# A decoder block on one core: bias row written reversed, modulation bias summed in, three steps of one sum on TensorE, weight places reordered

## What is computed

```
mod = silu(c) @ w_ada + b_ada                  # six rows of 1024: sh1, sc1, g1, sh2, sc2, g2
h   = x * (1 + sc1) + sh1
q, k, v = h @ w_in                             # 8 heads of block attention, 8 of dilated attention
y   = concat(rms(attention_a), rms(attention_b)) @ w_out    # every logit gets a bias by distance
x   = layer_norm(ALPHA * x + (1 + g1) * y)
h2  = x * (1 + sc2) + sh2
# PEER: 8 query heads per token, product keys, 16 experts per head
f   = sum over the 128 experts of a token of  gelu(h2 . u_e) * g_e * v_e
out = layer_norm(ALPHA * x + (1 + g2) * f)
```

## Time and profile before

| | |
|---|---|
| time before, median of 3 runs | 843.8 us (842.85 to 845.88) |
| time of the profiled execution | 842.22 us |
| its span in the trace | 840.4 us |
| busy share: TensorE, VectorE, ScalarE, GpSimd | 85%, 67%, 41%, 34% |
| moved by DMA | 327.95 MB, 390 GB/s over the span |
| chain of waits that ended last | DMA of expert rows 43%, TensorE 35%, VectorE 9% |

### The profile page before, as it was taken

How to read it: one execution, slowest core, us unless ns; L and a number is a source line. 1 busy time by engine, 2 the same in 40 slices (tenths; PEclk the granted TensorE clock), 3 DMA queues, 4 the chain that set the end, 5 groups by cost and what they waited for, 6 DMA issues and landing times.

```text
span 840.4 us, 7310 instructions
## 1 busy us (share of the span) xinstructions
PE 712.5 (85%) x2042; PEld 339.2 (40%) x2042; DVE 567.0 (67%) x1289; ACT 343.8 (41%) x998; POOL 286.3 (34%) x260
## 2 busy tenths in 40 slices
PE   5999999889999989998987876887787787878784
PEld 2876854645545535543432322332222222223221
DVE  6775776679768577756666667767576767675445
ACT  0032032266736444435453436343434435343333
POOL 0000000133534435444544443534343444435420
PEclk9999999899999999999999999999999999999999
DMA  9999993299999999999999999999999999999991
GB/s 353 402 421 422 391 414 112 82 375 411 381 413 418 421 420 421 422 421 420 423 421 420 423 421 422 422 420 423 420 421 422 421 422 422 421 422 406 422 422 74
DMA packets 48183, 327.95 MB, mean 390 GB/s; under 512 B 5584, under 2 KB 7952, under 8 KB 9232
## 3 DMA queue, kind: packets, MB, share of 16 engines
q0 software_dynamic: 36864, 268.45, 77.3%
q1 hardware_dynamic: 10544, 58.73, 17.3%
q10 hardware_dynamic: 736, 0.32, 0.1%
HBM read 326.40 MB, written 1.07 MB: 390 GB/s over the span
## 4 chain that ended last, share of the span: by engine, by line
DMA 46%; PE 35%; DVE 9%; ACT 6%; issue 3%; SPq 1%; ACTq 0%; DVEq 0%; POOL 0%
DMA ring<-in_experts,e_all 43%; PE bank L447 19%; PE bank L439 8%; DVE ring L767 4%; PE bank L470 3%; DMA ring<-in_w 3%; DVE acc L870 2%; ACT diag L617 2%; PE bank L544 1%; ACT weight L613 1%; PE bank L525 1%; ACT L609 1%; PE bank L581 1%; SPq L352 1%; PE bank L515 1%
## 5 line engine op out<-in xcount | busy, mean ns | idle before, releaser
L447 PE MATMUL bank<-ring,diag 128*128 128x512 f32 x1024 | 499.3, 623 | 97.6 <-ACT diag L617 97.4
L987 POOL DMA_INDIRECT ring<-in_experts,e_all x256 | 286.1, 1117 | 526.7 <-PE bank L447 341.4
L447 PEld LDWEIGHTS bank<-ring,diag 128*128 128x128 f32 x1024 | 183.9, 194 | 389.7 <-ACT diag L617 225.6
L767 DVE CUSTOM_DVE_ANT_0 ring<-ring,T_h 128x1024 f32<-128x1024 f32 x128 | 156.7, 1225 | 113.4 <-DMA ring<-in_experts,e_all 113.4
L767 DVE CUSTOM_DVE_ANT_0 ring<-ring,h 128x1024 f32<-128x1024 f32 x128 | 156.6, 1224 | 96.0 <-DMA ring<-in_experts,e_all 95.8
L609 ACT ACTIVATE gel<-pre 128x1 f32<-128x1 f32 x256 | 51.8, 203 | 327.3 <-DVE pre L767 326.6
L617 ACT ACTIVATE diag<-consts,weight 128x128 f32<-128x128 f32 x256 | 102.8, 401 | 8.4
L613 ACT ACTIVATE weight<-gel,g_all 128x1 f32<-128x1 f32 x256 | 75.4, 295 | 9.3
L870 DVE SCALAR_TENSOR_TENSOR acc<-ring,cact,acc 128x512 f32<-128x512 f32 x70 | 52.6, 752 | 3.2
L439 PE MATMUL bank<-ring,hT_yT 128*128 128x512 f32 x80 | 39.9, 655 | 1.7 <-DMA ring<-in_w 1.6
L470 PE MATMUL bank<-hT_yT,lnw 128*128 128x256 f32 x128 | 31.0, 404 | 1.1 <-DVE hT_yT L846 1.1
(11 more groups left out here) (150 smaller groups left out, 527.2 us busy)
## 6 DMA issues: line engine op xcount, KB each, us to landing
ring<-in_w SPq DMA_DIRECT2D x30, 1024.0 KB, 14.5
lnw<-in_w SPq DMA_DIRECT2D x6, 1024.0 KB, 16.7
ring<-in_experts,e_all POOLq DMA_INDIRECT x256, 15.0
H_s<-in_w SPq DMA_DIRECT2D x3, 1024.0 KB, 25.3
mod<-in_w SPq DMA_DIRECT2D x2, 1024.0 KB, 26.6
H_s<-scratch SPq DMA_DIRECT2D x1, 2048.0 KB, 26.6
mod<-in_b_ada_r SPq DMA_DIRECT2D x1, 2048.0 KB, 23.3
lnw<-in_ln SPq DMA_DIRECT2D x1, 2048.0 KB, 11.1
```

Of the source, the lines that this page charges most:

```text
L447: last = nc.tensor.matmul(tile_sum(t)[n], diag[:, i % DIAGS, :], ring[:, RING_AT[i], D + CH * n:D + CH * n + CH], start=(s == 0), stop=(s ...
L767: nc.vector.tensor_tensor_reduce(ring[:, r, 0:D], ring[:, r, 0:D], h2[i // SLOTS], 1.0, 0.0, ALU.mult, ALU.add, pre[:, i % PAIR:i % PAIR + ...
L987: nc.gpsimd.indirect_dma_start(ring[:, r, :], None, A["experts"], bass.IndirectOffsetOnAxis(ap=e_all[:, i:i + 1], axis=0)).then_inc(slot_i ...
```

## The change

- **Bias by distance.** VectorE writes the row reversed, the read back starts one element later and goes straight to `toep`, and VectorE reads `toep` backwards along its last axis. The eight `tflip` matmuls and ScalarE's eight copies are gone.
- **Modulation bias.** GpSimd clears `mod`; a 16 KB DMA puts b_ada in partition 0; GpSimd adds 1 to three of its rows. The first step of each sum from chunk 4 on adds that row (a SCALAR_TENSOR_TENSOR in place of a TENSOR_SCALAR), so the sum over partitions contains it once. The step `madd` becomes a copy on ScalarE.
- **Chunk ada 2.** Its slices 3, 6 and 7 leave VectorE. TensorE multiplies them as they are, with the matching column of `cact` as moving operand, 12 matmuls (`modk`) into the bank of `modc` 0, which is opened by one matmul of zeros.
- **Places and order.** `mod` is no longer a place; `H_s` is. Chunks, loads and steps have a new order. ScalarE issues its small loads later, most of them after the bias row is written.

```diff
@@ -66,18 +66,19 @@
 EXP_PIECE = 7
 
 
-STREAM = [("ada", 0), ("ada", 2), ("in", 0), ("ada", 1), ("ada", 3), ("in", 1), ("ada", 4), ("ada", 5), ("ada", 6), ("in", 2),
-          ("in", 3), ("ada", 7), ("in", 4), ("ada", 8), ("ada", 9), ("in", 5), ("out", 0), ("ada", 10), ("out", 1), ("q", 0),
+STREAM = [("ada", 0), ("ada", 2), ("in", 0), ("ada", 1), ("ada", 3), ("in", 1), ("ada", 4), ("in", 2), ("in", 3), ("ada", 5),
+          ("in", 4), ("ada", 6), ("ada", 7), ("ada", 8), ("ada", 9), ("in", 5), ("out", 0), ("ada", 10), ("out", 1), ("q", 0),
...
-LN_PLACE, MOD_PLACE, HANKEL_PLACE = 4, 5, 6
-W_PLACES = [0, 1, LN_PLACE, 2, 3, MOD_PLACE, 3, 1, 2, 0, 3, 1, LN_PLACE, HANKEL_PLACE, 2, 1, 2, 3, LN_PLACE, 3]
+LN_PLACE, H_PLACE = 4, 5
+W_PLACES = [0, 1, LN_PLACE, 2, 3, H_PLACE, 1, 0, 2, 3, LN_PLACE, H_PLACE, 1, 3, H_PLACE, 2, 1, 3, LN_PLACE, 3]
...
+BY_PE = {2: (3, 6, 7)}
...
+NARROW = [4, 5, 6, 7, 0, 1]
+WIDE = [2, 3] + NARROW
...
-    [("qkz", 0, 0), ("qkz", 0, 1), ("qkz", 1, 0), ("wsum", 0), ("bias",), ("qkz", 1, 1), ("modp", 0), ("wsum", 2), ("modc", 0), ("qkh", 0, 0), ("qkh", 0, 1), ("wsum", 1), ("modp", 1),
-       ("qkh", 1, 0), ("wsum", 3), ("modc", 1), ("qkh", 1, 1), ("qk", 0, 0), ("qk", 0, 1), ("qk", 1, 0), ("qk", 1, 1), ("wsum", 4)]
-    + [("tflip", j) for j in range(8)]
-    + [("wsum", 5), ("wsum", 6), ("S", 0), ("S", 1), ("v", 0, 0), ("wsum", 7), ("Tr", 0), ("Tr", 1), ("qk", 2, 0), ("PV", 0), ("PV", 1),
-       ("modrow", 0), ("madd", 0), ("modrow", 1), ("madd", 1), ("modrow", 2), ("madd", 2), ("wsum", 8), ("qk", 2, 1), ("yT", 0, 0),
-       ("wsum", 9), ("qk", 3, 0), ("modrow", 3), ("madd", 3), ("modrow", 4), ("madd", 4), ("qk", 3, 1), ("wsum", 10), ("S", 2), ("S", 3),
-       ("v", 1, 0), ("wsum", 11), ("modrow", 5), ("madd", 5), ("Tr", 2), ("Tr", 3), ("wo", 0, 0, 0), ("PV", 2), ("PV", 3), ("ny", 0),
+    [("qkz", 0, 0), ("qkz", 0, 1), ("qkz", 1, 0), ("wsum", 0), ("bias",), ("qkz", 1, 1), ("modp", 0)] + [("modk", 2, k) for k in BY_PE[2]]
+    + [("wsum", 2), ("modc", 0), ("qkh", 0, 0), ("qkh", 0, 1), ("wsum", 1), ("modp", 1),
+       ("qkh", 1, 0), ("wsum", 3), ("modc", 1), ("qkh", 1, 1), ("qk", 0, 0), ("qk", 0, 1), ("qk", 1, 0), ("qk", 1, 1), ("wsum", 4),
+       ("S", 0), ("S", 1), ("v", 0, 0), ("wsum", 5), ("qk", 2, 0), ("Tr", 0), ("Tr", 1), ("modrow", 0), ("madd", 0), ("PV", 0), ("PV", 1),
+       ("wsum", 6), ("qk", 2, 1), ("modrow", 1), ("madd", 1), ("yT", 0, 0), ("wsum", 7), ("qk", 3, 0), ("modrow", 2), ("madd", 2), ("wsum", 8),
+       ("modrow", 3), ("madd", 3), ("qk", 3, 1), ("wsum", 9), ("S", 2), ("S", 3), ("modrow", 4), ("madd", 4), ("v", 1, 0), ("wsum", 10),
+       ("modrow", 5), ("madd", 5), ("Tr", 2), ("Tr", 3), ("wo", 0, 0, 0), ("wsum", 11), ("PV", 2), ("PV", 3), ("ny", 0),
...
-        yT = [part.rearrange("p (k c) -> p k c", k=KC) for part in (H_s[:, D:2 * D], hT_yT[:, 0:D])]
...
-        nought = T_h2[0:1, 0:CH]
         h2_0 = sb("h2_0", [P, D])
+        yT = [part.rearrange("p (k c) -> p k c", k=KC) for part in (h2_0[:], hT_yT[:, 0:D])]
...
-        places = [wring[:, n] for n in range(WRING)] + [tile[:].rearrange("p r (k n) -> p (r k) n", n=CH) for tile in (lnw, mod)]
+        places = [wring[:, n] for n in range(WRING)] + [tile[:].rearrange("p r (k n) -> p (r k) n", n=CH) for tile in (lnw,)]
...
-        patches = [tile.rearrange("p (k n) -> p k n", n=CH) for tile in (h2_0[:], xT_y[:, D:2 * D], H_s[:, 0:D], V_x1[:, 1, :])]
...
+        nought = acc[0:1, 3, :]
...
-        consts = sb("consts", [P, 2 * P + TOPK])
-        ident, flip, iota = consts[:, 0:P], consts[:, P:2 * P], consts[:, 2 * P:2 * P + TOPK]
+        consts = sb("consts", [P, P + TOPK])
+        ident, iota = consts[:, 0:P], consts[:, P:P + TOPK]
...
             sp.wait_ge(biasrow_out, 16)
-            shifts = bass.AP(A["scratch"].tensor, 0, [[1, P], [ROW, NH], [1, T]])
-            sp.dma_start(hankel, shifts).then_inc(hankel_in, 16)
-            summed(sp, 2)
+            shifts = bass.AP(A["scratch"].tensor, 1, [[1, P], [ROW, NH], [1, T]])
+            sp.dma_start(toep, shifts).then_inc(hankel_in, 16)
+            filled(sp, ("modc", 0))
+            load(("ada", 4))
+            summed(sp, 0)
+            load(("in", 2))
+            summed(sp, 1)
+            load(("in", 3))
             summed(sp, 3)
-            load(("ada", 4))
             load(("ada", 5))
-            load(("ada", 6))
-            load(("in", 2))
-            summed(sp, 4)
-            load(("in", 3))
-            summed(sp, 5)
-            load(("ada", 7))
             filled(sp, ("qk", 0, 1))
             load(("in", 4))
             filled(sp, ("qk", 1, 1))
-            sp.dma_start(mod[:].rearrange("p r c -> p (r c)"), A["b_ada_r"].broadcast_to([P, 4 * D])).then_inc(rows_in, 16)
-            filled(sp, ("tflip", 7))
+            load(("ada", 6))
+            summed(sp, 4)
+            load(("ada", 7))
+            summed(sp, 5)
             load(("ada", 8))
+            sp.dma_start(x[:], A["x"].rearrange("(t p) c -> p t c", p=P)).then_inc(x_in, 16)
             summed(sp, 6)
             load(("ada", 9))
+            filled(sp, ("qk", 2, 1))
+            load(("in", 5))
             summed(sp, 7)
-            load(("in", 5))
-            sp.dma_start(x[:], A["x"].rearrange("(t p) c -> p t c", p=P)).then_inc(x_in, 16)
+            load(("out", 0))
+            summed(sp, 8)
+            load(("ada", 10))
             summed(sp, 9)
-            load(("out", 0))
-            filled(sp, ("qk", 2, 1))
-            load(("ada", 10))
-            summed(sp, 8)
-            sp.dma_start(ln1.rearrange("p r c -> p (r c)"), A["ln"][:, 0:2 * D].broadcast_to([P, 2 * D])).then_inc(ln1_in, 16)
             sp.wait_ge(hT_ready, KC)
             last = A["w"][CHUNK[("ada", 11)]].rearrange("p (k n) -> p k n", k=KC)
             for i, patch in enumerate(patches):
                 sp.dma_start(patch, last[:, 2 * i:2 * i + 2]).then_inc(patch_in[i], 16)
             filled(sp, ("qk", 3, 1))
             load(("out", 1))
+            sp.dma_start(ln1.rearrange("p r c -> p (r c)"), A["ln"][:, 0:2 * D].broadcast_to([P, 2 * D])).then_inc(ln1_in, 16)
             summed(sp, 10)
             load(("q", 0))
...
 
                 summed(pe, c)
                 for j in range(4):
-                    last = nc.tensor.matmul(dst[:, 4 * c + j:4 * c + j + 1], acc[:, c, P * j:P * j + P], ones[:, 0:1], start=True, stop=True)
+                    last = nc.tensor.matmul(dst[:, 4 * c + j:4 * c + j + 1], acc[:, c, P * j:P * j + P], ones[:, 0:1],
+                                            start=not opened, stop=not opened or (c == 2 and j == 3))
                 return last
...
                 if kind == "modp":
                     pe.wait_ge(set_ready, 1)
-                    column_sums(open_bank(("modc", step[1]))[0], step[1])
+                    dst, _ = open_bank(("modc", step[1]))
+                    if step[1] == 0:
+                        nc.tensor.matmul(dst[:, 0:2 * KC], nought[:, 0:P], nought[:, 0:2 * KC], start=True, stop=False)
+                    column_sums(dst, step[1], step[1] == 0)
+                if kind == "modk":
+                    c, k = step[1:]
+                    n = CHUNK[("ada", c)]
+                    arrived(pe, n, 2 * k // KC)
+                    pe.wait_ge(cact_ready, 1)
+                    for j in range(4):
+                        nc.tensor.matmul(bank[PLACE[("modc", 0)][0]][:, 4 * c + j:4 * c + j + 1], places[W_PLACES[n]][:, k, P * j:P * j + P],
+                                         cact[:, k:k + 1], start=False, stop=False)
...
-                elif kind == "tflip":
-                    pe.wait_ge(consts_in, 16)
-                    pe.wait_ge(hankel_in, 16)
-                    nc.tensor.matmul(dst[:], flip, H_s[:, CH * step[1]:CH * step[1] + CH], start=True, stop=True).then_inc(full, 1)
...
-            nc.scalar.dma_start(badac[:], A["b_ada_c"]).then_inc(badac_in, 16)
             for name, dst in (("relT", relT[:]), ("onehot", onehot), ("maskrow", maskrow)):
                 nc.scalar.dma_start(dst, A[name]).then_inc(bias_in, 16)
-            nc.scalar.dma_start(consts[:], A["consts"]).then_inc(consts_in, 16)
-            nc.scalar.dma_start(gn[:], A["gn"]).then_inc(gnsk_in, 16)
-            nc.scalar.dma_start(skT[:], A["skT"]).then_inc(gnsk_in, 16)
             act.wait_ge(set_ready, 1)
             act.wait_ge(c_in, 16)
             nc.scalar.activation(ctanh[:], cin[:], ACT.Tanh, scale=0.5).then_inc(tanh_ready, 1)
+            nc.scalar.dma_start(badac[:], A["b_ada_c"]).then_inc(badac_in, 16)
+            act.wait_ge(rows_zero, 1)
+            nc.scalar.dma_start(mod[0:1].rearrange("p r c -> p (r c)"), A["b_ada_r"]).then_inc(rows_in, 16)
             settle_bank(act, ("bias",))
             nc.scalar.dma_start(A["scratch"], biasrow).then_inc(biasrow_out, 16)
+            nc.scalar.dma_start(ident, A["consts"][:, 0:P]).then_inc(consts_in, 16)
```

(62 more changed lines are left out.)

13 lines of the change are left out of this document (5 added, 8 removed).

## The result

The changed kernel takes 838.01 us (median of 20 runs, 834.7 to 842.67), the kernel before 844.09 us (20 runs). The ratio is 0.9929, with a 95% interval from 0.9916 to 0.9942: **6.0 us faster**, where 6.6 were forecast. The profiled execution took 836.12 us, against 842.22 before, and its span is 834.3 us.

The account below looks back on a forecast made before the run. TensorE bounds the first stage from 64.6 us, with DMA-bound second stage unchanged; -6.2 + 4.0 - 1.6 - 1.7 - 1.1 = -6.6, so 842.2 becomes 835.6 profiled, 837.2 us median; range 832.8 to 841.0.

Parts of the forecast that it names:

- Turning dropped, -6.2: TensorE before the logits: eight bias-turning matmuls, 7.03 us, go; the logits then wait 0.8 for a copy; net -6.2 us.
- the copy that I had named: ScalarE's last copy of the k projection, ending 0.8 us after the matmuls; the logits would wait for it.
- Three steps on TensorE, +4.0: Chunk ada 2: TensorE does three slices before its column sums, so the projection starts 4.0 us later, at 26.2.
- the slow of the two prices: Twelve new small matmuls on TensorE: 5.6 us at the low clock, taken, against 2.9 at the fast one.
- Chunk in 2 earlier, -1.6: Value projection of group 0: chunk in 2 lands at 54.6, before it is due at 60.9; no wait, -1.6 us.
- no slow clock behind it, -1.7: Value projection on TensorE: without the wait the clock dip goes, 8 matmuls having taken 8.80 against 7.03 or 7.13; -1.7 us.
- Transposes no longer waiting, -1.1: Two transposes at 119 on TensorE no longer wait 0.18 and 0.91 us for ScalarE's exponentials; -1.1 us.
- Two us to spare, so DMA hides behind TensorE, narrowly.: Weight stream: out 1 lands at 117.1, TensorE wants it at 119.5, so no wait for it.
- a bubble of a us or two: SP's loads wait for sums 6 to 9; called fed, with a gap of a us or two possible.
- No row prices its work: GpSimd's adding of 1 to three rows, 3072 columns: 2.8 us at VectorE's rate, with some 25 us available.
- GpSimd gets in VectorE's way: Rival, chance 0.12: GpSimd's adds in sums 1 or 3 stall VectorE 0 to 2.8 us; result 837.2 to 840.0.
- The idle stretch from 17 to 25: VectorE has nothing to do from 17 to 25 us, called the likeliest time for GpSimd's adds.

Follow-up runs that it names:

- the first experiment: Kernel before with only the turning dropped (bias row written reversed, eight matmuls and copies gone), loads in the old order: 844.29 us, ratio 1.0015.
- the last pair of runs: Changed kernel with sums 6 and 7 earlier, adds on ScalarE, x loaded after out 1: 835.28 us with TensorE's three steps, 832.07 with chunk ada 2 all on VectorE.

## Why the prediction was right

The time came out at 838.01 against 837.2, and by the ratio 6.0 us were gained of 6.6. The path is the forecast one: the gain lies on TensorE in the first stage and arrives at the first gather. That the total came this close is partly luck. The traces show 5.1 us in the first stage; the 1.0 us in the second was not in the sum, and nothing here shows that it belongs to the change. Term by term:

- *Turning dropped, -6.2.* Between the end of the projection (58.1) and the logits (58.92) lies the copy that I had named, 0.77. Right, but the first experiment shows that the term can't stand by itself: alone it is worth nothing (ratio 1.0015).
- *Three steps on TensorE, +4.0.* Measured +3.9: 5.26 for the twelve (5.6 taken, from the slow of the two prices), 0.44 for the opening (0.3 taken), and 0.7 for the bias row, which VectorE delivered late (TensorE goes on at 14.11 instead of 13.40). By their spacing (219 ns per record, 119 behind dense matmuls) the small matmuls ran at the low clock throughout. Two errors offset each other here, and the figure names one cause where there were two: with the three steps taken away the projection still starts at 26.09, because GpSimd holds up VectorE's sum as long. Without GpSimd's adds the steps cost 3.3 us (25.28 against 22.00), and 2.7 in the last pair of runs. That the forecast of 26.2 fits is luck in that respect.
- *Chunk in 2 earlier, -1.6, and no slow clock behind it, -1.7.* Both as forecast: no wait at 60.53, 7.13 us.
- *Transposes no longer waiting, -1.1.* Right: they follow the matmul before them at 112.9 without a wait.
- *"Two us to spare, so DMA hides behind TensorE, narrowly."* This step failed, by 1.9 us. I had computed the landing at 117.1 from the bytes alone and noted that a bubble of a us or two was possible; out 1 came at 121.0, 3.9 us later. The sum should have had it as a term: SP's waits for sums 6 and 9 were in the text, with 85 against 87 and 105 against 107, a margin of 2 us, with which the stream still thinned to 293 and 350 GB/s.
- *GpSimd.* "No row prices its work": the 2.8 us, taken from VectorE's rate, was too low by a factor of three (8.6), and the adds began at 11, not 18. So the rival "GpSimd gets in VectorE's way" did happen, in sums 0 and 2. The idle stretch from 17 to 25 that I gave as the reason against it is what hid 3.3 us of it; 0.7 came through.

On TensorE the first stage gained 5.1 us: 6.6 less the 1.95 of waiting, and 0.4 that the small terms return.

## What to carry to other kernels

Removing work from an engine only counts if what the engine needs next is there earlier too: at each removed block, write down when the data for the next block lands. Where a DMA queue waits in order for a consumer, compare the moment of the wait with the moment when the queued bytes run out, and ask for some us of margin, since a gap is paid by everything behind it. Work moved to an idle engine is not free for that reason alone: GpSimd's adds held up VectorE's sum by 3.3 us, and the slices given to TensorE stood in front of TensorE's own next step. The two costs found here hid each other, so removing either alone gained almost nothing; only the run with both removed showed them.
